# Modulation transposes and first norm sums queued later against the planner's model; constants in TensorE's first waits

## What is computed

```python
mod = jnp.einsum('bd,ldm->lbm', jax.nn.silu(c), w_mod) + b_mod[:, None, :]
for i in range(DEPTH):                      # 2 layers
    sh_m, sc_m, g_m, sh_f, sc_f, g_f = [t[:, None, :] for t in jnp.split(mod[i], 6, axis=-1)]
    h = x * (1.0 + sc_m) + sh_m
    y = even_mixer(...) if i % 2 == 0 else odd_mixer(...)
    x = layer_norm(ALPHA * x + (1.0 + g_m) * y, ln_mix_g[i], ln_mix_b[i])
    h = x * (1.0 + sc_f) + sh_f
    y = swiglu(h, w_gate[i], w_up[i], w_down[i])
    x = layer_norm(ALPHA * x + (1.0 + g_f) * y, ln_ffn_g[i], ln_ffn_b[i])
```

## Time and profile before

| what | us |
|---|---|
| median of 3 runs | 1166.73 |
| the runs | 1165.50, 1166.73, 1170.66 |
| the profiled execution | 1167.61 |
| its span | 1166.3 |
| PE busy | 1128.5 |
| DVE busy | 839.1 |
| ACT busy | 629.3 |

### The profile page before, as it was taken

One profiled execution on the slowest core, in us unless ns is written; L12 is line 12 of the kernel. 1 busy time (PEld: TensorE's weight loads), 2 busy tenths in 40 slices (PEclk: granted clock), 3 DMA queues, 4 the chain that ended last, 5 costly groups with the idle time before them and its releaser, 6 DMA issues.

```text
span 1166.3 us, 24932 instructions
## 1 busy us (share of the span) xinstructions
PE 1128.5 (97%) x10510; PEld 1080.8 (93%) x10510; DVE 839.1 (72%) x1427; ACT 629.3 (54%) x1075; POOL 77.5 (7%) x101
## 2 busy tenths in 40 slices
PE   5999989999998999999999999999999999999998
PEld 4988879999998999998999999999999999999987
DVE  4688779888885688797566569768656667776743
ACT  2378536544443677666444454744655557565542
POOL 3000012000000200120000004400000000000000
PEclk8999999999999999999999999999999999999999
DMA  9963866988997544546646552744245554656550
GB/s 315 347 220 109 297 210 222 305 299 290 325 306 261 197 145 145 182 145 207 222 154 209 185 180 73 236 163 147 74 145 181 173 180 136 197 176 206 182 179 37
DMA packets 194687, 232.22 MB, mean 199 GB/s; under 512 B 4083, under 2 KB 169555, under 8 KB 194576
## 3 DMA queue, kind: packets, MB, share of 16 engines
q1 hardware_dynamic: 193984, 230.32, 59.6%
q0 software_dynamic: 592, 0.31, 0.2%
HBM read 229.56 MB, written 1.05 MB: 198 GB/s over the span
## 4 chain that ended last, share of the span: by engine, by line
PE 86%; DVE 8%; issue 2%; ACT 1%; DMA 1%; POOL 0%; SPq 0%; DVEq 0%; ACTq 0%
PE ps L154 85%; DVE wlo L187 2%; PE ps L157 2%; DMA MW<-in_w_mod_dram 1%; DVE hL L196 1%; DVE T L187 1%; DVE first L187 1%; DVE LT L196 1%; DVE LT L187 0%; DVE Fg L196 0%; POOL T L187 0%; DVE T L196 0%; ACT LT L166 0%; DVE XA L193 0%; ACT T L166 0%
## 5 line engine op out<-in xcount | busy, mean ns | idle before, releaser
L187 DVE TENSOR_TENSOR wlo<-raw,whi 128x1024 fp32r<-128x1024 f32 (+1 forms) x346 | 408.0, 1201 | 162.8 <-ACT whi L166 161.1
L154 PE MATMUL ps<-hH,whi 128*128 128x256 f32 (+3 forms) x1792 | 517.7, 289 | 3.6 <-DVE hL L187 2.2
L154 PE MATMUL ps<-hH,wlo 128*128 128x256 f32 (+3 forms) x1792 | 506.5, 283 | 6.1 <-DVE wlo L187 6.1
L154 PE MATMUL ps<-hL,whi 128*128 128x256 f32 (+3 forms) x1792 | 506.3, 283 | 0.0
L166 ACT ACTIVATE whi<-raw 128x1024 fp32r<-128x1024 f32 (+1 forms) x346 | 349.6, 1033 | 201.8 <-PE ps L154 141.3
L154 PEld LDWEIGHTS ps<-hH,whi 128*128 128x128 f32 x1792 | 339.2, 189 | 9.9 <-issue 6.5
L154 PEld LDWEIGHTS ps<-hH,wlo 128*128 128x128 f32 x1792 | 339.4, 189 | 7.4 <-DVE wlo L187 7.4
L154 PEld LDWEIGHTS ps<-hL,whi 128*128 128x128 f32 x1792 | 339.8, 190 | 0.3
L154 PE MATMUL ps<-uL,whi 128*128 128x256 f32 x352 | 99.2, 282 | 0.0
L154 PE MATMUL ps<-uH,whi 128*128 128x256 f32 x352 | 99.0, 281 | 0.0
L154 PE MATMUL ps<-uH,wlo 128*128 128x256 f32 x352 | 98.4, 280 | 0.0
(11 more groups left out here) (312 smaller groups left out, 1631.7 us busy)
## 6 DMA issues: line engine op xcount, KB each, us to landing
MW<-in_w_mod_dram SPq DMA_DIRECT2D x47, 1024.0 KB, 6.2
raw<-in_w_up_dram SPq DMA_DIRECT2D x44, 1024.0 KB, 5.5
raw<-in_w_in_dram SPq DMA_DIRECT2D x36, 1024.0 KB, 5.0
raw<-in_w_down_dram SPq DMA_DIRECT2D x27, 1024.0 KB, 5.6
raw<-in_w_gate_dram SPq DMA_DIRECT2D x22, 1024.0 KB, 7.2
raw<-in_w_in_odd_dram SPq DMA_DIRECT2D x12, 1024.0 KB, 5.2
raw<-in_w_in_even_dram SPq DMA_DIRECT2D x8, 1024.0 KB, 8.0
raw<-in_w_down_dram SPq DMA_DIRECT2D x8, 768.0 KB, 6.5
```

The lines of the kernel that those rows point to most:

```text
L154: return self.queued(self.e.matmul(out, lhsT, rhs, start=start, stop=stop, skip_group_check=True, **kw), length if pos is None else max(le ...
L187: return self.queued(self.e.tensor_tensor(out, a, b, op), 0.07 + cols(out) / self.RATE)
```

## The change

Five places. `LATER`, 0.8 us of the planner's time, is added to what a modulation transpose waits for, to the sums of DVE's pieces, to the bank's time for pieces from the ninth on, and to the partial sums of the norms behind the mixers. `modulated` waits for the scale's modulation beside the shift's. `keep_clock` puts matmuls of constants with constants into the start: 1, 3 and 5 around the transposes of `c` and the bias, 2 and 1 behind the first two pieces, 4 after the first two blocks are modulated; their result in bank 0 is not read.

```diff
@@ -55,6 +55,7 @@
 
 
 FIRST_MODS = 8
+LATER = 0.8
 BY_VECTOR = {18, 19, *range(22, 38), 46, 47}
 MODS = [(0, ch, s) for s in range(4) for ch in (1, 0)] + [(0, ch, s) for ch in (2, 4, 3, 5) for s in range(4)]
 MODS += [(1, ch, s) for ch in (1, 0, 2, 4, 3, 5) for s in range(4)]
@@ -683,6 +684,13 @@
 
 
 
+def keep_clock(k, n):
+
+    ones = k.m.ones.rearrange("p a n -> p (a n)")
+    for _ in range(n):
+        k.pe.mm(k.m.ps[0][:, 0:256], ones[:, 0:128], ones[:, 0:256], True, True)
+
+
 def begin(k):
     pe, act, dve, pool, sp, m, D_ = k.pe, k.act, k.dve, k.pool, k.sp, k.m, k.D
     RV = m.RV
@@ -719,12 +727,16 @@
 
 
     fill(k, 4, 5, 6)
+    pe.wait_ge(*k.ones_done)
+    keep_clock(k, 1)
     c_turned = pe.wait_ge(*c_in).wait_ge(*ident_in).tr(m.ps[4][:, 0:8], RV[0:8, 0, :], ident[0:8, 0:8]).inc()
     silu = act.wait_ge(*c_turned).act(m.ST[:, 0:8], m.ps[4][:, 0:8], ACT.Silu).inc()
     k.silu_c = dve.wait_ge(*silu).copy(m.SC32, m.ST[:, 0:8].unsqueeze(2).to_broadcast([128, KD, 32])).inc()
 
+    keep_clock(k, 3)
     bm_turned = pe.wait_ge(*bm_in).tr(m.ps[5][:, 0:96], RV[0:96, 1, :], ident[0:96, 0:96]).inc()
     bm = dve.wait_ge(*bm_turned).copy(m.V[:, 0:96], m.ps[5][:, 0:96]).inc()
+    keep_clock(k, 5)
     dve.settle()
     for l in range(2):
         for ch in (1, 4):
@@ -874,7 +886,7 @@
     def bank_of(n):
         while MODS[n] not in k.mod:
             yield None
-        yield due(k.mod[MODS[n]])
+        yield due(k.mod[MODS[n]]) + (0.0 if n < FIRST_MODS else LATER)
 
     for n, (l, ch, s) in enumerate(MODS):
         b = n if n < len(k.m.MW) else n % 2
@@ -928,6 +940,8 @@
             at = 256 * c + g % 2 * 128
             pe.mm(ps[32 * g:32 * g + 32, 0:128], m.SC32[:, c, :], m.MW[b][:, at:at + 128], i == 0, i == 3, pos=(0, 32 * g))
     k.mod_sums[n] = pe.inc()
+    if n < 2:
+        keep_clock(k, 2 - n)
     if k.first_loads:
         load_first(k)
     elif n >= FIRST_MODS - 2:
@@ -985,7 +999,7 @@
         yield from spare(k)
     more_mods(k)
     if s % 2:
-        yield due(k.mod_sums[n])
+        yield due(k.mod_sums[n]) + LATER
 
         pe.wait_ge(*k.mod_sums[n])
         for g in range(4):
@@ -999,7 +1013,7 @@
     l, ch, s = MODS[n]
     yield due(sums)
     row = dve.wait_ge(*sums).copy(m.MR[:, 0:128], m.ps[3][:, 0:128]).inc()
-    yield due(row)
+    yield due(row) + LATER
     k.turned = pe.wait_ge(*row).tr(m.ps[3][:, 128:256], m.MR[:, 0:128], m.CST[:, K_ID:K_ID + 128]).inc()
     yield due(k.turned)
     c0 = l * 48 + ch * 8 + s // 2 * 4
@@ -1017,10 +1031,10 @@
 
     act, dve, m = k.act, k.dve, k.m
     t = m.LT[:, 256 * j:256 * j + 256]
-    shift = (0, 0, j // 2)
-    pace(k, lambda: due(k.mod[shift]) if shift in k.mod else None)
-
-    x = dve.wait_ge(*k.x_cols[j]).wait_ge(*k.mod[shift]).ts(t, t, mod_columns(k, 0, 1, j, 1), ALU.mult, mod_columns(k, 0, 0, j, 1), ALU.add).inc()
+    scale, shift = (0, 1, j // 2), (0, 0, j // 2)
+    pace(k, lambda: due(k.mod[scale], k.mod[shift]) if scale in k.mod and shift in k.mod else None)
+
+    x = dve.wait_ge(*k.x_cols[j]).wait_ge(*k.mod[scale]).wait_ge(*k.mod[shift]).ts(t, t, mod_columns(k, 0, 1, j, 1), ALU.mult, mod_columns(k, 0, 0, j, 1), ALU.add).inc()
     hi = act.wait_ge(*x).act(m.hH[:, j, TOK], t, ACT.Copy).inc()
     k.h_low[j] = dve.wait_ge(*hi).tt(m.hL[:, j, TOK], t, m.hH[:, j, TOK].bitcast(F32), ALU.subtract).inc()
 
@@ -1037,6 +1051,8 @@
     for s in range(4):
         modulated(k, 2 * s)
         modulated(k, 2 * s + 1)
+        if s == 0:
+            keep_clock(k, 4)
         jobs = []
         for i, w in enumerate(widths):
             bank, n, wide = banks[i // 2], i % 2, i >= 4
@@ -1602,10 +1618,10 @@
     else:
         part = dve.settle().tt(acc, acc, T(6), ALU.add).inc()
         total = pool.wait_ge(*squared[6]).settle().tt(sqa, sqa, sq[6], ALU.add).inc()
-        yield due(part)
+        yield due(part) + LATER
     alone = where[6][0] != where[7][0]
     pe.wait_ge(*part).mm(mean, ones[:, 0, :], acc, alone, False)
-    yield due(total)
+    yield due(total) + (LATER if alone else 0.0)
     pe.wait_ge(*total).mm(var, ones[:, 0, :], sqa, alone, False)
     yield from arrived(7)
     residual(7)
```

## The result

The changed kernel takes 1171.44 us (median of 10 runs, 1168.72 to 1173.05), the kernel before 1167.20 (10 runs, 1163.68 to 1170.66) on the same chip: the ratio is 1.0034, 95% interval 1.0021 to 1.0046. It is slower by 4 us, where 1161.2 was forecast with 1156.5 to 1168.5 as the range. By the bound of 0.5% this is still "the same".

What follows compares the result with a forecast made beforehand. PE was taken as the bound, busy for 1128.5 of 1166.3 us. The terms -2.0 + 0.3 - 3.5 - 0.3 = -5.5 gave 1162.1 us for the profiled run and 1161.2 for the median, range 1156.5 to 1168.5.

Steps and rivals of the forecast that it cites:

- A: Front: constants keep the clock up, gaining 2.9 us, of which later `hL` takes 0.9; -2.0 us, bounds -2.9 and 0.
- the dear case: Front: sixteen constant matmuls at the lower clock's 0.64 us each, 10.2 us of work.
- the other case: Front: sixteen constant matmuls at the median 0.38 us each, 6.1 us of work.
- Rival (1): Front: the clock falls all the same at about 21 us; total -3.5, 1163.2 us; chance 0.2.
- B: Attention, 60 to 160 us: reordering costs only stalls from later scores; +0.3 us, bounds -0.8 and +3.
- near the rows that show full cover: Attention: reason for choosing +0.3 us, as the fourth group's scores-to-product way was covered by matmuls and modulation pieces.
- rival (3): Attention: fourth sparse group's late scores push the last product up to 6.4 + 2 us later; 1169.6 us; chance 0.1.
- C: First layer norm: products moved ahead, weights restart 7.4 us after the projection's end, one `wlo` less; -3.5 us, bounds -4.5 and -1.0.
- D: Second layer's norm: first sums queued later against a wait of 1.2, mostly given back; -0.3 us, bounds -1.2 and 0.
- Rival (2): Norm: delays do nothing wanted, DVE as late as before, front gain half eaten; 1165.2 us; chance 0.2.

Runs made afterwards that it cites:

- e3: The changed kernel without the constant matmuls, delays alone (LATER 0.8): 1165.23 us, ratio 0.9990 to before.
- e11: The kernel before plus uncounted constants, no delays, leaving out the one ahead of the transposes of x and the four behind them: 1167.01 us, ratio 1.0002.
- e2: The changed kernel with LATER = 0: constants counted in the planner's clock, no delays; 1162.91 us, ratio 0.9967 to before.
- e1: The kernel before plus all sixteen constant matmuls, not counted in the planner's clock, no delays: 1163.36 us, ratio 0.9976.
- e10: The changed kernel with the planner's split condition loosened for one unit, putting the sixth split back ahead of `first`: 1167.40 us, ratio 1.0012 to before.
- e8: The changed kernel without LATER on the modulation sums that DVE's products feed: 1168.12 us, ratio 1.0007 to before.
- e12: The kernel before plus only the four constant matmuls ahead of the first weights, uncounted, no delays: 1164.75 us, ratio 0.9985.
- e6: The changed kernel with the load of modulation piece 23 cut to 1/16 of its bytes: 1171.72 us, ratio 1.0038 to before.
- e7: The changed kernel with the load of modulation piece 23 issued later, behind the load of `raw` 21: 1170.42 us, ratio 1.0028 to before.

## Why the prediction was wrong, step by step

**A, the front: the mechanism was right, the size too small.** The clock is 1.00 at 21 to 27.5, and PE is 2.6 us ahead of before at the 24th weight matmul, near the 2.9 of the forecast. Not all of this is sure in each execution: in e3, without constants, the clock is 0.74 in this window, and PE is 1.6 ahead there. The sixteen take 10.9 us in all, about the 10.2 of the dear case. The 0.38 of the other case is the length of one record of the earlier trace rows, and a matmul of constants stands as two, so that four take 1.99 at the full clock. Their cover holds: the first piece starts at 10.84 (10.37 before), the first weight matmul at 20.39 (20.70). The 0.9 that the later `hL` of the second quarter was to take back did not occur: at the 240th matmul, near 60 us, the change is still 2.66 ahead (59.34 against 62.00). The first `hL` stands at 32.99, not at 34.3, as PE and all before it were earlier too, which the working left out:

```profile
32.99 0.42 DVE L188 TENSOR_TENSOR hL<-LT,hH 128x256 fp32r<-128x256 f32 x1 [0.48 <-ACT hH L167]
```

The transfer hole at 35 us closed as said (share 1.02 against 0.19). Rival (1) did not happen. In e11 PE does nothing but transposes from 14.5 to 17.7 us, at a granted 1.00 throughout, and the clock falls only at 21.7, behind the idle time; in before the rate rises while PE transposes. The Trainium skill's page "TensorE: Matmul & The Clock Gate", section "Part 4: PE-mode transpose", says that transposes don't count as PE work for the clock gate; these two traces speak against it for fp32 transposes. No run has transposes alone for longer than 3.2 us, so a fall that only comes late is not ruled out.

**B, attention: wrong in size, with little effect on the end.** E was to come at 159.1; it comes 1.36 later than before though PE entered 2.66 ahead, so up to here the order costs 4.0, not 0.3, beyond even the bound of +3. The forecast said that the end moves only by stalls, and took the number of covering matmuls for proof that none would come. The stalls are 2.25, 1.80 and 1.71, on ACT's and DVE's results. The step that failed is "near the rows that show full cover": the rows were of the old order, and matmuls between two instructions on PE cover nothing if ACT and DVE have been given other work between them. It was no part of rival (3) either: the fourth group's last product comes at 146.62, 2.7 later than before, not 8.4. But this loss mostly doesn't reach the end. Over the thirteen profiles E spreads from 156.5 to 165.2, 8.7 us, and the end of the wait for `wlo` only from 194.0 to 197.1, as DVE is the limit in between. e2 has the late E and the lowest ratio of all.

**C, the norm: right up to the restart, with the wrong sign behind it.** R is 169.33 - 162.12 (161.84 and one matmul of 0.28) = 7.2 behind the end of the projection, 7.4 was forecast, 9.5 it was the earlier trace rows. Then the working took "one `wlo` of 1.21 less before PE's wait" at 196.41 as 1.2 us gained through DVE. That is the step that turned the sign. The `wlo` is not saved, it is moved behind `first`, and PE's work that needs it moves along. DVE reaches `first` no earlier (at 190.78, 189.89 in before; the wait ends 0.3 later), and PE comes out of it with 42 matmuls more to do. The forecast asked when the wait would end and not how much PE would have done by then; the earlier trace rows showed a wait of 1.58 behind a full queue of matmuls, so any split taken from ahead of it could only make it longer. Term C was -3.5 and is, from the wait's end on, +0.3 + 5.0 + 0.7 = +6.0 at 230 us, with all that A and B had brought already lost in it. It is not the whole of the miss. The forecast was 0.47% below before and the measurement is 0.34% above it; putting the sixth split back returns 0.22 to 0.27 of these 0.81%. e2, which has no delays, is at 0.9967 and so near the forecast: the rest went with the delays, B and D among it, and is in part open.

**The way to the end.** Of the 5.95 at 230 us, 5.91 are still there at the sums of the norm at the end of the first layer (375.83 against 369.92), and 2.7 at those of the second layer's first (502.34 against 499.60). The row of the first, and the window behind it, in the profile of the change:

```profile
375.83 1.46 PE L155 MATMUL ps<-LT,ones 128*128 128x256 f32 x6
```

```profile
375.00:392.00 17.00, 14.36 (x207) 12.51 (x199) 12.10 (x31) 8.37 (x17) 4.44 (x5) 1.00 0.77 273
```

The granted clock of this window is 1.00, where the profile of before has 0.80: 0.2 x 17 = 3.4 us (an estimate). Nothing of the change stands there, and the other kernels lie between (0.88 in e1, 0.92 in e2, 0.94 in e10), so I take it for a difference of single executions, not for a gain of the change; no run tests that. With it the profiled runs are 2.8 apart, the medians 4.2.

**D, the second layer's norm: the wrong sign.** The wait of 1.2 for `LT` is gone, and 0.3 of gain was forecast. But the order with the delays brings two new waits, of 0.55 and 1.47, and over the whole norm PE loses 0.8 us: between the same two weight matmuls (at 496.89 and 532.88 in before), with the same work between them, before takes 35.99 us, the change 36.77 and e8 36.75, all three at the full clock. The longest waits of the change from 460 to 535 are:

```profile
PE ps L155 <- DVE wlo L188: 2.6, 2, 2.5
PE ps L155 <- DVE hL L197: 1.5, 1, 1.5
PE ps L155 <- DVE T L197: 0.5, 1, 0.5
```

**The rivals.** Rival (2), that the delays do nothing wanted, is near the truth for the delays alone (e3, 0.9990), though not by its mechanism: the wait for the partial sum does go, and one for the products takes its place. The case that happened, slower by a split taken from ahead of DVE's long stretch and by more waits with the delays, was not among the rivals, and the range ended 2.9 us short of it.

## What to carry to other kernels

Where one engine feeds another and is about to be busy with something else for some microseconds, count how much work of the second lies ready ahead of that stretch; an operation moved from before it to behind it is no gain for the first and can be a loss for the second, by up to all the work that hangs on it. Filler that a planner counts in its modelled clock reorders everything behind it: add it uncounted first, and look at the two effects apart (here 0.9976 and 0.9967, but 1.0034 together with a delay that alone did nothing). A pause of an engine that runs at the lower clock behind it is worth covering, and a few matmuls right over the pause may do as much as many ahead of it. And before two profiles are compared, their stretches at the lower clock have to be: e2's and e10's end 1.4 us apart, their ratios to before 5.2.

## What the runs showed of the hardware

Four fp32 matmuls of constants, 128x256, over an idle stretch of about 2 us kept the granted clock at 1.00 in the window behind it (e12), where it was 0.50 before; it then stood through a wait of 0.77, in the change through one of 1.10. In e11 the same sort of wait, 1.10, ended 1.6 us behind an idle stretch of 2.23 that nothing covered, and the clock was 0.62 behind it. Sixteen transposes of 128x128 in fp32 ran in 2.00 us at 1.00. Four matmuls of constants, 128x256 in fp32, took 1.99 us at the full clock and stand as eight records. A pause alone does not decide it: after PE's wait of 2.25 at 111 us the clock stayed at 1.00 in the profiles of the change (110 to 160) and of e10, and was 0.83 to 0.86 from 105 to 115 in those of e6, e7 and e8, whose E is 3.2 us later. What makes the difference between these was not found.
